# A chunked RWKV-7 recurrence: the triangular inverses and their products kept as 64x64 diagonal blocks, and grams of three slots

## The chip, the cores and the metric

The kernel runs on one core of one Trainium2 chip. The metric is the device time of one execution in microseconds (us), the median of several runs.

## What is computed

One layer of a hybrid streaming encoder for 1024 tokens of width 1024: input projection, a latent attention group, an RWKV-7 group, output projection, cross attention over 256 memory tokens, and a product-key expert stage. The change touches the RWKV-7 group alone. Of the reference, that is the scan below; each of its 8 heads has a state of 64x64 (the gates, decays and the group norm around it are left out here):

```python
def step(state, inp):
    r_t, w_t, k_t, v_t, kk_t, a_t = inp
    sa = jnp.einsum('bhvk,bhk->bhv', state, kk_t)
    state = (state * w_t[:, :, None, :]
             - sa[..., None] * (kk_t * a_t)[:, :, None, :]
             + v_t[..., None] * k_t[:, :, None, :])
    return state, jnp.einsum('bhvk,bhk->bhv', state, r_t)
```

## The kernel before

The program is a row of stages with a barrier of all engines between them, so the time of a stage is a part of the whole time. Inputs pass through input projection, the attention group, `rwkv_stage`, output projection, cross attention and the expert stage. Only `rwkv_stage` and its constant masks matter here.

`rwkv_stage` works on 8 tiles of 128 tokens. A tile holds two chunks of 64 tokens (CH) and 8 heads, as four pairs (PAIRS, index f) of an even and an odd head (index e). The scan over a chunk is turned into matrix products: for each head a lower triangular 64x64 matrix L has to be inverted, (I+L)^-1. The two chunks of a tile sit as the two diagonal blocks of a 128x128 matrix, whose other two blocks are zero, and all products are made on the 128x128 matrix.

A tile has two parts on each engine. `matrices` transposes four operands on TensorE (L980), then makes per head a "gram" of four 128x128 slots (L997, L999), which VectorE masks into `gm` (L1358) with `mask4`; its slot 2 keeps the pairs of neighbours alone, and from it the first step of the inverse is read (L1367). It makes the triangular matrix again, turned (L1006), which VectorE masks into `lb` (L1365) and into `yi` (L1374), then the bonus sum (L1013) and the products `ux` (L1018). ScalarE copies `ux` out (L1170).

`solve` doubles the inverted block size in five levels, l = 1 to 5. `xi` is the inverse (turned) and `yi` the same, unturned. Each level has three products per head: p = lb.xi (L1032), which ScalarE copies to `pe_s` (L1179); then z = yi.pe_s (L1048) and, but for the last level, its turned twin (L1051). VectorE copies from z the places of this level into `xi` (L1387, a copy under a mask) and from the twin into `yi` (L1389). The even heads (e = 0) and the odd heads (e = 1) go one behind the other: while ScalarE copies the even half, TensorE makes the odd one.

```python
for e in range(2):
    w.wait("p_taken", 2 * (l - 1) + e + 1)
    w.wait("inv_t", 2 * (l - 1) + e + 1)
    for f in range(PAIRS):
        last = nc.tensor.matmul(bank[2 + e][:, f, :], yi[e][:, f, :], pe_s[e][:, f, :], ...)
        if l < 5:
            last = nc.tensor.matmul(bank[4 + e][:, f, :], pe_s[e][:, f, :], yi[e][:, f, :], ...)
    inc(last, "z_mm")
```

After the levels, L1060 multiplies the inverse by the right sides, ScalarE copies the result to `nu` (L1189), L1068 to L1087 make what the states need, and L1094 and L1103 step the state through the two chunks. Every engine runs a program of its own, written out by hand, and waits on semaphores; `each_tile` loops over the tiles. The next tile's elementwise work (`prepare`, steps 0 to 6) is hung between the levels: TensorE makes step 1 (L952, L956) behind level 2 and step 3 (L963) in level 4, VectorE makes step 2 (L1301 to L1313) behind level 3 and step 4 (L1318 to L1331) behind level 5. GpSimd presets `yi` (L1263), makes the masks `level_t` when the stage begins (L1231 to L1243) and norms the tile before (L1217 to L1227).

All operands are float32. One matmul of the program shows as two LDWEIGHTS and two MATMUL records in the trace; "records" below are these. A form such as 64*128 128x128 names the rows and columns of the array that are in use, then partitions and columns of the moving operand.

## Time and profile before

| | us |
|---|---|
| median of 3 runs | 4144.01 |
| lowest and highest run | 4128.92, 4152.92 |
| the profiled execution's own time | 4149.77 |
| its span | 4148.2 |
| TensorE busy over the span | 3733.1 (90%) |
| VectorE, GpSimd, ScalarE busy | 2736.3, 1926.8, 1250.3 |

The trace gives the start and length of every instruction of one execution; a matmul's end is modelled, so lengths of matmuls overlap, and the distance between starts is what one costs. "Idle before" names what an engine waited for. PEclk is the granted clock of TensorE: 1.00 is the higher of its two levels (2.4 GHz) and 0.50 the lower (1.2 GHz).

### The profile page before, as it was taken

How to read it: one execution, taken by the hardware profiler on the slowest of the kernel's cores; microseconds unless marked ns; L12 is line 12 of the kernel's file. 1: busy time of each engine (PE TensorE's matmuls, PEld its weight loads, DVE VectorE, ACT ScalarE, POOL GpSimd, SP SyncE). 2: the span in 40 equal slices, each digit the busy share in tenths (PEclk: the TensorE clock that was granted, in tenths of full speed). 3: DMA queues.
4: the chain of work that ended last, by engine and by line, in shares of the span. 5: the costliest groups of instructions: out<-in, count | busy, mean ns of one | idle time of the engine just before them, and what ended most of it. 6: DMA issues, size and time to landing. Idle time of an engine off the chain costs nothing.

```text
span 4148.2 us, 54997 instructions
## 1 busy us (share of the span) xinstructions
PE 3733.1 (90%) x19168; PEld 3180.8 (77%) x19168; DVE 2736.3 (66%) x5219; ACT 1250.3 (30%) x1836; POOL 1926.8 (46%) x1352
## 2 busy tenths in 40 slices
PE   6958879999779789999999999999879988999998
PEld 5834468888667577889989999999657777778877
DVE  5453367777204437847778888878797655689986
ACT  2013234333102312133323333333233322433333
POOL 2004022222001001887878888888888888022220
PEclk9979889999899899999999999999989999999999
DMA  2229500000220023548878888888879888899995
GB/s 97 100 95 397 215 24 18 18 9 9 81 102 31 16 75 96 92 92 248 256 242 266 259 265 258 263 259 251 218 208 270 259 246 253 290 380 389 388 375 195
DMA packets 376334, 788.59 MB, mean 190 GB/s; under 512 B 137104, under 2 KB 245648, under 8 KB 342288
## 3 DMA queue, kind: packets, MB, share of 16 engines
q1 hardware_dynamic: 210320, 451.28, 31.9%
q0 software_dynamic: 165888, 336.01, 27.4%
q14 instruction: 93, 0.76, 0.1%
q8 instruction: 33, 0.54, 0.1%
HBM read 643.09 MB, written 144.05 MB: 190 GB/s over the span
## 4 chain that ended last, share of the span: by engine, by line
POOL 30%; PE 14%; issue 8%; DMA 4%; DVE 4%; ACT 1%; DVEq 1%; SPq 0%; POOLq 0%; ACTq 0%
POOL gates_d L2000 26%; PE peer_ps L2111 5%; PE peer_ps L2033 4%; PE peer_ps L2019 3%; DMA late_in<-gates_d 3%; POOL rows L1980 2%; POOL peer_rows L1980 2%; POOL late_rows L1980 1%; DVE late_rows L2389 1%; PE peer_ps L2057 1%; DVE peer_acc L2404 1%; DVEq L2403 1%; DMA rows<-in_expert_uv,peer_idx 1%; DMA peer_gat<-gates_d 1%; DMA peer_rows<-in_expert_uv,peer_idx 1%
## 5 line engine op out<-in xcount | busy, mean ns | idle before, releaser
L2000 POOL DMA_INDIRECT gates_d<-peer_gates,peer_idx x768 | 1343.9, 1750 | 325.8 <-issue 224.3
L2019 PE MATMUL peer_ps<-high,peer_uh 128*128 128x384 f32 x2048 | 532.5, 341 | 60.1 <-DVE peer_ul L2306 52.5
L2019 PE MATMUL peer_ps<-high,peer_ul 128*128 128x384 f32 x2048 | 527.3, 338 | 0.0
L2019 PE MATMUL peer_ps<-low,peer_uh 128*128 128x384 f32 x2048 | 527.2, 338 | 0.0
L2019 PEld LDWEIGHTS peer_ps<-high,peer_uh 128*128 128x128 f32 x2048 | 373.3, 191 | 73.5 <-issue 65.2
L2111 PE MATMUL peer_ps<-peer_vh,peer_ah 128*128 128x512 f32 x1026 | 331.4, 405 | 59.0 <-DVE peer_al L2423 58.4
L2019 PEld LDWEIGHTS peer_ps<-low,peer_uh 128*128 128x128 f32 x2048 | 376.5, 191 | 0.0
L2019 PEld LDWEIGHTS peer_ps<-high,peer_ul 128*128 128x128 f32 x2048 | 376.2, 191 | 0.0
L1980 POOL DMA_INDIRECT late_rows<-in_expert_uv,peer_idx x108 | 141.8, 1313 | 430.1 <-DVE peer_acc L2404 389.0
L2111 PE MATMUL peer_ps<-peer_vh,peer_al 128*128 128x512 f32 x1026 | 324.7, 398 | 0.0
L2111 PE MATMUL peer_ps<-peer_vl,peer_ah 128*128 128x512 f32 x1026 | 324.0, 398 | 0.0
L2157 ACT ACTIVATE peer_uh<-peer_raw 128x1024 fp32r<-128x1024 f32 x144 | 152.2, 1057 | 515.5 <-PE peer_ps L2019 436.1
L2111 PEld LDWEIGHTS peer_ps<-peer_vh,peer_ah 128*128 128x128 f32 x1026 | 194.4, 194 | 116.3 <-DVE peer_al L2423 75.5
L2111 PEld LDWEIGHTS peer_ps<-peer_vh,peer_al 128*128 128x128 f32 x1026 | 198.1, 193 | 43.7
L2111 PEld LDWEIGHTS peer_ps<-peer_vl,peer_ah 128*128 128x128 f32 x1026 | 197.6, 193 | 43.2
L2306 DVE TENSOR_TENSOR peer_ul<-peer_raw,peer_uh 128x1024 fp32r<-128x1024 f32 x144 | 177.2, 1230 | 78.6 <-ACT peer_uh L2157 62.8
L2111 PE MATMUL peer_ps<-peer_uh,peer_ah 128*128 128x512 f32 x510 | 165.1, 405 | 30.2 <-DVE peer_al L2423 29.7
L2196 ACT ACTIVATE peer_pre<-peer_pre 128x2 f32<-128x2 f32 x128 | 26.0, 203 | 516.3 <-DVE peer_pre L2389 512.8
L2389 DVE CUSTOM_DVE_ANT_0 late_rows<-late_rows,peer_xrow 128x1024 f32<-128x1024 f32 x108 | 128.3, 1219 | 60.3 <-DMA late_rows<-in_expert_uv,peer_idx 60.3
L2111 PE MATMUL peer_ps<-peer_uh,peer_al 128*128 128x512 f32 x510 | 163.0, 401 | 0.0
L2111 PE MATMUL peer_ps<-peer_ul,peer_ah 128*128 128x512 f32 x510 | 162.6, 400 | 0.0
L2404 DVE SCALAR_TENSOR_TENSOR peer_acc<-late_rows,peer_pre,peer_acc 128x1024 f32<-128x1024 f32 x108 | 138.8, 1285 | 9.5 <-issue 0.5
(442 smaller groups left out, 7609.6 us busy)
## 6 DMA issues: line engine op xcount, KB each, us to landing
late_in<-in_expert_uv SPq DMA_DIRECT2D x170, 512.0 KB
gates_d<-mla_zeros POOLq DMA_DIRECT2D x128, 512.0 KB
peer_raw<-in_expert_u SPq DMA_DIRECT2D x128, 512.0 KB
hidden_d<-peer_hid SPq DMA_DIRECT2D x128, 384.0 KB
peer_val<-in_expert_uv SPq DMA_DIRECT2D x86, 512.0 KB
late_in<-hidden_d SPq DMA_DIRECT2D x170, 192.0 KB
late_in<-gates_d SPq DMA_DIRECT2D x170, 192.0 KB
peer_act_in<-hidden_d SPq DMA_DIRECT2D x86, 192.0 KB
```

Source lines behind the costliest of these rows:

```text
L1980: pool.indirect_dma_start(buffer[:, :], None, expert_uv, bass.IndirectOffsetOnAxis(ap=idx[:, n, k:k + 1], axis=0)).then_inc(ready, 16)
L2000: pool.indirect_dma_start(gates_flat, bass.IndirectOffsetOnAxis(ap=idx[:, n, k:k + 1], axis=0), gates[:, n, k:k + 1], None, compute_op=ALU ...
L2019: last = nc.tensor.matmul(ps[i][:, a, 0:HD], w[:, cols], x[:, kc, a * HD:(a + 1) * HD], start=(kc == 0 and w is uh[i % 2] and x is high), ...
L2033: last = nc.tensor.matmul(ps[i][:, a, :], w[:, cols], x[:, kc, a * HALF:(a + 1) * HALF], start=(kc == 0 and w is uh[i] and x is high), sto ...
L2057: last = nc.tensor.matmul(ss[:, t, :], q[j % 2][:, t * P:(t + 1) * P], keys[:, j, :], start=True, stop=True)
L2111: last = nc.tensor.matmul(ps[n % 4][:, a, :], x[:, i * P:(i + 1) * P], w[:, a * HALF:(a + 1) * HALF], start=(first_block and x is ah[r] an ...
L2157: nc.scalar.activation(uh[b % 2][:, :], raw[b % 3][:, :], ACT.Copy).then_inc(u_high, 1)
L2196: nc.scalar.activation(pre[:, part], pre[:, part], ACT.Gelu).then_inc(gel_done, 1)
L2306: nc.vector.tensor_tensor(ul[b % 2][:, :], raw[b % 3][:, :], uh[b % 2][:, :].bitcast(F32), ALU.subtract).then_inc(u_low, 1)
L2389: nc.vector.tensor_tensor_reduce(out=buffer[:, 0:D], in0=buffer[:, 0:D], in1=xrow[row_place(p)[0]][:, :], scale=1.0, scalar=0.0, op0=ALU.m ...
L2403: dve.drain()
L2404: nc.vector.scalar_tensor_tensor(out=acc[tile][:, :], in0=rows(p)[0][:, D:2 * D], scalar=pre[:, p:p + 1], in1=acc[tile][:, :], op0=ALU.mul ...
```

## The change

`lb`, `xi`, `yi` and `pe_s` hold only the two diagonal blocks: 64 columns per head in place of 128, chunk 0 on partitions 0 to 63 and chunk 1 on 64 to 127. A product of a level is made as 16 matmuls of 64x64x64 in place of 8 of 128x128x128. A block of chunk c uses rows and columns 64c to 64c+63 of the array; `ROUNDS` puts a block of the even heads on one quarter beside a block of the odd heads on the quarter diagonal to it, each in a bank of its own. The even and the odd half are no longer staggered: one semaphore step per product. All `xi` copies of a level stand ahead of all `yi` copies. The gram has three slots (its second matmul has 128 columns in place of 256), and the first step of the inverse is read from a product of its own (`turned`). `level`, `lower` and `unit` are cut to blocks by GpSimd when the stage begins, and GpSimd presets `xi` too.

```diff
+        def in_bank(e, low=0):
+            return bank[e][:, low:low + 2, :].rearrange("p a (g c) -> p (a g) c", c=CH)
+        def chunk(c):
+            return slice(CH * c, CH * c + CH)
+        ROUNDS = (((0, 0), (1, 1)), ((0, 1), (1, 0)))
...
-                    inc(nc.tensor.matmul(bank[2 + h % 4][:, 2:4, :], bh[rows, f, :], ktrt[rows, f, :, :],
+                    inc(nc.tensor.matmul(bank[2 + h % 4][:, 2, :], bh[rows, f, :], ktrt[rows, f, 1, :],
...
                 for e in range(2):
-                    rows = slice(64 * e, 64 * e + 64)
                     w.wait("trans_taken", 3 + e)
+                pe.nop().then_inc(operands_seen, 1)
+                for turned in range(2):
                     for f in range(PAIRS):
-                        last = nc.tensor.matmul(bank[6 + e][:, f, :], ktrt[rows, f, 0, :], bh[rows, f, :],
-                                                start=True, stop=True)
+                        for c in range(2):
+                            for e in range(2):
+                                rows = slice(64 * e, 64 * e + 64)
+                                x, y = ktrt[rows, f, 0, chunk(c)], bh[rows, f, chunk(c)]
+                                last = nc.tensor.matmul(in_bank(6 + e, 2 * turned)[chunk(c), f, :], y if turned else x,
+                                                        x if turned else y, start=True, stop=True)
                     inc(last, "lb_mm")
...
+                def blocks(dst, x, y):
+                    pe.nop().then_inc(operands_seen, 1)
+                    for pair in ROUNDS:
+                        for f in range(PAIRS):
+                            for e, c in pair:
+                                rows = chunk(c)
+                                last = nc.tensor.matmul(in_bank(dst + e)[rows, f, :], x[e][rows, f, :], y[e][rows, f, :],
+                                                        start=True, stop=True)
+                    return last
...
-                    for e in range(2):
-                        w.wait("p_taken", 2 * (l - 1) + e + 1)
-                        w.wait("inv_t", 2 * (l - 1) + e + 1)
-                        for f in range(PAIRS):
-                            last = nc.tensor.matmul(bank[2 + e][:, f, :], yi[e][:, f, :], pe_s[e][:, f, :],
-                                                    start=True, stop=True)
-                            if l < 5:
-                                last = nc.tensor.matmul(bank[4 + e][:, f, :], pe_s[e][:, f, :], yi[e][:, f, :],
-                                                        start=True, stop=True)
-                        inc(last, "z_mm")
+                    w.wait("p_taken", 2 * l)
+                    w.wait("inv_t", 2 * l)
+                    inc(blocks(2, yi, pe_s), "z_mm")
+                    if l < 5:
+                        inc(blocks(4, pe_s, yi), "z_mm")
...
-                    for f in range(PAIRS):
-                        last = nc.tensor.matmul(bank[e][:, f, :], xi[e][:, f, :], rhsU[:, 2 * f + e, :],
-                                                start=True, stop=True)
-                    inc(last, "u_mm")
+                    for f in range(PAIRS):
+                        for e, c in pair:
+                            rows = chunk(c)
+                            last = nc.tensor.matmul(bank[e][rows, f, :], xi[e][rows, f, :], rhsU[rows, 2 * f + e, :],
+                                                    start=True, stop=True)
+                inc(last, "u_mm")
...
-                        inc(nc.scalar.activation(flat(pe_s[e]), flat(bank[e]), ACT.Copy), "p_taken")
+                        inc(nc.scalar.activation(pe_s[e][:, :, :], in_bank(e), ACT.Copy), "p_taken")
...
-                gv = gm[:, :, :, :].rearrange("p (f e) w c -> p f e w c", e=2)
+                w.wait("lb_mm", 2)
                 for e in range(2):
-                    w.wait("lb_mm", e + 1)
-                    inc(nc.vector.tensor_tensor(lb[e][:, :, :], bank[6 + e][:, :, :], over_heads(consts["lower"][:, :]),
-                                                ALU.mult), "lb")
-                    inc(nc.vector.tensor_tensor(xi[e][:, :, :], gv[:, :, e, 2, :], over_heads(consts["ident"][:, :]),
-                                                ALU.add), "inv")
+                    inc(nc.vector.tensor_tensor(lb[e][:, :, :], in_bank(6 + e), over_blocks(lower[:, :]), ALU.mult), "lb")
+                w.wait("preset", 4)
+                dve.nop().then_inc(blocks_seen, 1)
+                for e in range(2):
+                    inc(nc.vector.copy_predicated(xi[e][:, :, :], where(level_t, 0), in_bank(6 + e, 2)), "inv")
...
+                    for n, (dst, masks, src, done) in enumerate(((xi, level_t, 2, "inv"), (yi, level, 4, "inv_t"))):
+                        if l == 5 and n:
+                            continue
+                        w.wait("z_mm", 2 * l - 1 + n)
+                        dve.nop().then_inc(blocks_seen, 1)
+                        for e in range(2):
+                            inc(nc.vector.copy_predicated(dst[e][:, :, :], where(masks, l), in_bank(src + e)), done)
```

How the instructions stand. First TensorE in level 4 of the loop over tiles: p, then step 3 of the next tile, then the start of z and its twin. Before (a row without "x" is one matmul of the program):

```order
L1032 MATMUL rwkv_bank<-rwkv_xi,rwkv_lb 128x128 [waits rwkv_inv]
L1032 MATMUL rwkv_bank<-rwkv_xi,rwkv_lb 128x128 x3
L902 REGISTER_ALU
L1032 MATMUL rwkv_bank<-rwkv_xi,rwkv_lb 128x128 [waits rwkv_inv]
L1032 MATMUL rwkv_bank<-rwkv_xi,rwkv_lb 128x128 x3
L902 REGISTER_ALU
L963 MATMUL rwkv_bank<-rwkv_sqk,headones 128x512 [waits pin_rstd_ready,pin_scaled_ready]
L902 REGISTER_ALU
L1048 MATMUL rwkv_bank<-rwkv_pe_s,rwkv_yi 128x128 [waits rwkv_inv_t,rwkv_p_taken]
L1051 MATMUL rwkv_bank<-rwkv_yi,rwkv_pe_s 128x128
```

The same place in the changed kernel, to the end of the twin:

```order
L1046 MATMUL rwkv_bank<-rwkv_xi,rwkv_lb 64x64 [waits rwkv_inv]
L1046 MATMUL rwkv_bank<-rwkv_xi,rwkv_lb 64x64 x15
L912 REGISTER_ALU
L973 MATMUL rwkv_bank<-rwkv_sqk,headones 128x512 [waits pin_rstd_ready,pin_scaled_ready]
L912 REGISTER_ALU
L1046 MATMUL rwkv_bank<-rwkv_pe_s,rwkv_yi 64x64 [waits rwkv_p_taken,rwkv_inv_t]
L1046 MATMUL rwkv_bank<-rwkv_pe_s,rwkv_yi 64x64 x15
L1046 MATMUL rwkv_bank<-rwkv_yi,rwkv_pe_s 64x64 x16
```

Each product is now 16 small matmuls behind one wait; z stands whole ahead of its twin.

Second, VectorE behind level 3, with step 2 of the next tile and the copies of level 4. Before:

```order
L1387 COPY_PREDICATED rwkv_xi<-rwkv_level_t,rwkv_bank 128x512 [waits rwkv_z_mm]
L1389 COPY_PREDICATED rwkv_yi<-level,rwkv_bank 128x512
L1301 SCALAR_TENSOR_TENSOR rwkv_cum<-scanmask,rwkv_sgw 128x512 [waits pin_sq_summed]
L1303 TENSOR_TENSOR rwkv_prev<-rwkv_cum,rwkv_sgw 128x512
L1305 TENSOR_TENSOR rwkv_rem<-rwkv_cum 128x512
L1310 SCALAR_TENSOR_TENSOR rwkv_ta<-rwkv_al,cols 128x512 [waits pin_sq_summed]
L1313 SCALAR_TENSOR_TENSOR rwkv_k<-rwkv_ta,rwkv_rkv 128x512
L902 REGISTER_ALU
L1387 COPY_PREDICATED rwkv_xi<-rwkv_level_t,rwkv_bank 128x512 [waits rwkv_z_mm]
```

And in the changed kernel:

```order
L1415 COPY_PREDICATED rwkv_xi<-rwkv_level_t,rwkv_bank 128x256 [waits rwkv_z_mm]
L1415 COPY_PREDICATED rwkv_xi<-rwkv_level_t,rwkv_bank 128x256
L912 REGISTER_ALU
L1415 COPY_PREDICATED rwkv_yi<-rwkv_level,rwkv_bank 128x256 [waits rwkv_z_mm]
L1415 COPY_PREDICATED rwkv_yi<-rwkv_level,rwkv_bank 128x256
L1329 SCALAR_TENSOR_TENSOR rwkv_cum<-scanmask,rwkv_sgw 128x512 [waits pin_sq_summed]
L1331 TENSOR_TENSOR rwkv_prev<-rwkv_cum,rwkv_sgw 128x512
L1333 TENSOR_TENSOR rwkv_rem<-rwkv_cum 128x512
L1338 SCALAR_TENSOR_TENSOR rwkv_ta<-rwkv_al,cols 128x512 [waits pin_sq_summed]
L1341 SCALAR_TENSOR_TENSOR rwkv_k<-rwkv_ta,rwkv_rkv 128x512
L912 REGISTER_ALU
L1415 COPY_PREDICATED rwkv_xi<-rwkv_level_t,rwkv_bank 128x256 [waits rwkv_z_mm]
```

The copies have half the columns, and step 2 still stands whole between the copies of level 3 and those of level 4.

## Rows read from the trace of the kernel before

**Rows 1.** Busy time by stretch (stretch, length, PE, PEld, DVE, ACT, POOL)
```profile
570.00:1040.00 470.00, 443.41 (x3720) 404.81 (x3718) 339.47 (x464) 175.55 (x273) 115.83 (x100) 0.99 0.05 14
682.20:743.20 61.00, 57.09 (x482) 51.79 (x480) 45.77 (x62) 23.94 (x38) 16.25 (x14) 1.00 0.06 15
```
**Rows 2.** Timeline of TensorE, one tile (start, length, line, form, records)
```profile
664.04 1.16 PE L1068 MATMUL rwkv_bank<-rwkv_br_t,rwkv_nu 64*128 64x128 f32 x8 [0.69 <-ACT rwkv_nu L1189]
...
673.46 1.10 PE L1094 MATMUL rwkv_bank<-rwkv_q,rwkv_state 128*128 128x64 f32 x8 [1.31 <-DVE rwkv_q L1406]
...
682.72 0.71 PE L997 MATMUL rwkv_bank<-rwkv_ktrt,rwkv_kh 64*128 64x256 f32 x4
...
691.07 2.16 PE L1032 MATMUL rwkv_bank<-rwkv_xi,rwkv_lb 128*128 128x128 f32 x16
...
698.01 2.38 PE L1032 MATMUL rwkv_bank<-rwkv_xi,rwkv_lb 128*128 128x128 f32 x16 [0.32 <-DVE rwkv_xi L1387]
...
705.88 2.05 PE L1032 MATMUL rwkv_bank<-rwkv_xi,rwkv_lb 128*128 128x128 f32 x16
...
711.40 2.26 PE L1032 MATMUL rwkv_bank<-rwkv_xi,rwkv_lb 128*128 128x128 f32 x16
...
717.99 2.39 PE L1032 MATMUL rwkv_bank<-rwkv_xi,rwkv_lb 128*128 128x128 f32 x16
722.21 2.11 PE L1060 MATMUL rwkv_bank<-rwkv_rhsU,rwkv_xi 128*128 128x128 f32 x16
725.01 1.16 PE L1068 MATMUL rwkv_bank<-rwkv_br_t,rwkv_nu 64*128 64x128 f32 x8 [0.69 <-ACT rwkv_nu L1189]
```
**Rows 3.** Timeline of TensorE: narrow matmuls, and matmuls on parts of the array
```profile
666.38 0.27 PE L1073 MATMUL rwkv_bank<-rwkv_v_t,rwkv_kr_t 64*128 64x128 f32 x1
666.38 0.37 PE L1068 MATMUL rwkv_bank<-rwkv_br_t,rwkv_nu 64*128 64x128 f32 x1
...
669.26 1.09 PE L1081 MATMUL rwkv_bank<-rwkv_gm,rwkv_nu 128*64 128x128 f32 x16
...
689.34 1.89 PE L1018 MATMUL rwkv_bank<-rwkv_v_t,rwkv_gm 128*128 128x64 f32 x16
```
**Rows 4.** Weight loads by line and form (busy, mean ns of one)
```profile
L1060 PEld LDWEIGHTS rwkv_bank<-rwkv_rhsU,rwkv_xi 128*128 128x128 f32 x128 | 15.4, 191 | 1.4 <-DVE rwkv_xi L1387 1.4
...
L1085 PEld LDWEIGHTS rwkv_bank<-rwkv_gm,rwkv_v_t 128*64 128x64 f32 x128 | 10.5, 146 | 0.0
```
**Rows 5.** Timeline of ScalarE, the same tile
```profile
691.27 0.60 ACT L1170 ACTIVATE rwkv_rhsU<-rwkv_bank 128x512 f32<-128x512 f32 x1 [6.17 <-PE rwkv_bank L1018]
691.88 1.28 ACT L1179 ACT_TABLE_LOAD   x1
693.17 1.08 ACT L1179 ACTIVATE rwkv_pe_s<-rwkv_bank 128x512 f32<-128x512 f32 x2
```
**Rows 6.** Timeline of VectorE, the same tile
```profile
683.88 4.87 DVE L1358 TENSOR_TENSOR rwkv_gm<-rwkv_bank,mask 128x512 f32<-128x512 f32 x8 [3.13 <-PE rwkv_bank L999]
...
712.34 0.73 DVE L1389 COPY_PREDICATED rwkv_yi<-level,rwkv_bank 128x512 f32<-128x512 uint32 x1
...
717.17 0.76 DVE L1387 COPY_PREDICATED rwkv_xi<-rwkv_level_t,rwkv_bank 128x512 f32<-128x512 uint32 x1 [0.28 <-issue]
```
**Rows 7.** TensorE and its granted clock (next to last but two) where it fell
```profile
907.20:910.60 3.40, 2.71 (x26) 2.62 (x27) 3.30 (x2) 1.63 (x3) 2.04 (x2) 0.99 0.00 0
910.60:920.90 10.30, 10.30 (x76) 9.79 (x74) 8.61 (x12) 0.00 (x0) 2.05 (x2) 0.51 0.00 0
```
**Rows 8.** Timeline of TensorE in that tile
```profile
907.98 1.16 PE L1068 MATMUL rwkv_bank<-rwkv_br_t,rwkv_nu 64*128 64x128 f32 x8 [0.69 <-ACT rwkv_nu L1189]
...
920.89 1.10 PE L1094 MATMUL rwkv_bank<-rwkv_q,rwkv_state 128*128 128x64 f32 x8
```
**Rows 9.** Timeline of GpSimd as the stage begins
```profile
533.53 0.24 POOL L1243 TENSOR_SCALAR_AFFINE_SELECT rwkv_level_t<-rwkv_level_t 128x64 f32<-128x64 f32 x1
537.02 1.04 POOL L1205 TENSOR_TENSOR rwkv_kkr<-rwkv_rkv,cols 128x512 f32<-128x512 f32 x1 [3.25 <-DMA rwkv_gd<-feats_d]
```

More of the change, by code:

```diff
@@ L138, in _ @@
             nc.gpsimd.memset(low[:, :], 1.0).then_inc(made, 1)
-            nc.gpsimd.memset(m4[:, 2, :], 0.0).then_inc(made, 1)
-            n = 12
-            for i in (0, 1, 3):
+            n = 11
+            for i in range(3):
                 pool.wait_ge(made, n)
                 nc.gpsimd.affine_select(out=m4[:, i, :], in_=m4[:, i, :], compare_op=ALU.is_ge, fill=0.0,
-                                        base=-1 if i % 2 == 0 else 0, pattern=[[1, P]],
+                                        base=0 if i else -1, pattern=[[1, P]],
                                         channel_multiplier=-1).then_inc(made, 1)
@@ L848, in rwkv_stage, with blocks4 @@
         kr_t, br_t, v_t = (tile4(x) for x in ("kr_t", "br_t", "v_t"))
-        gm = st.sb("gm", [P, 2 * PAIRS, 4, P])
-        lb = [tile4(f"lb{e}") for e in range(2)]
-        xi = [tile4(f"xi{e}") for e in range(2)]
-        yi = [tile4(f"yi{e}") for e in range(2)]
-        level_t = st.sb("level_t", [P, 6, P])
+        gm = st.sb("gm", [P, 2 * PAIRS, 3, P])
+        def blocks4(name):
+            return st.sb(name, [P, PAIRS, CH])
+        lb, xi, yi, pe_s = ([blocks4(f"{x}{e}") for e in range(2)] for x in ("lb", "xi", "yi", "pe_s"))
+        level, level_t = st.sb("level", [P, 6, CH]), st.sb("level_t", [P, 6, CH])
+        unit, lower = st.sb("unit", [P, CH]), st.sb("lower", [P, CH])
         bonus_kept, gate_kept = tile4("bonus_kept"), tile4("gate_kept")
-        pe_s = [tile4(f"pe_s{e}") for e in range(2)]
         nu = st.sb("nu", [P, 2, 2 * PAIRS, 64])
@@ L1080, in solve @@
                     f, rows = h // 2, slice(64 * (h % 2), 64 * (h % 2) + 64)
-                    last = nc.tensor.matmul(bank[4][rows, f, :], nu[:, 0, h, :], gm[:, h, 3, :], start=True, stop=True)
+                    last = nc.tensor.matmul(bank[4][rows, f, :], nu[:, 0, h, :], gm[:, h, 2, :], start=True, stop=True)
                 inc(last, "q_mm")
@@ L1086, in solve @@
                                      start=(h < 2), stop=False, skip_group_check=True)
-                    nc.tensor.matmul(bank[5][rows, f, :], nu[:, 1, h, :], gm[:, h, 3, :],
+                    nc.tensor.matmul(bank[5][rows, f, :], nu[:, 1, h, :], gm[:, h, 2, :],
                                      start=False, stop=False, skip_group_check=True)
@@ new lines, in made @@
+                def made(ins):
+                    nonlocal n
+                    n += 1
+                    ins.then_inc(masks_made, 1)
+                    pool.wait_ge(masks_made, n)
+                for c in range(2):
+                    rows = chunk(c)
+                    made(nc.gpsimd.tensor_tensor(level[rows, :, :], consts["level"][rows, :, rows],
+                                                 ones[rows, 0:CH].unsqueeze(1).broadcast_to([CH, 6, CH]), ALU.mult))
+                    for dst, src in ((lower, consts["lower"]), (unit, consts["ident"])):
+                        made(nc.gpsimd.tensor_tensor(dst[rows, :], src[rows, rows], ones[rows, 0:CH], ALU.mult))
@@ new lines, in make_masks @@
+                made(nc.gpsimd.memset(level_t[:, :, :], 1.0))
+                for l in range(6):
+                    b = 1 << l
+                    for c in range(2):
+                        v = level_t[chunk(c), l, :].rearrange("p (j y) -> p j y", y=2 * b)
+                        made(nc.gpsimd.memset(v[:, :, 0:b], 0.0))
+                        for base, step in ((0, -1), (b - 1, 1)):
+                            made(nc.gpsimd.affine_select(out=v[:, :, b:2 * b], in_=v[:, :, b:2 * b], fill=0.0,
+                                                         compare_op=ALU.is_ge, base=base,
+                                                         pattern=[[2 * step * b, CH // (2 * b)], [0, b]],
+                                                         channel_multiplier=-step))
@@ L1260, in matrices @@
                 if before:
-                    before.wait("u_mm", 2)
-                for e in range(2):
-                    inc(nc.gpsimd.tensor_tensor(yi[e][:, :, :], over_heads(consts["ident"][:, :]),
-                                                over_heads(consts["ident"][:, :]), ALU.mult), "preset")
+                    before.wait("u_mm", 1)
+                for x in xi + yi:
+                    inc(nc.gpsimd.tensor_tensor(x[:, :, :], over_blocks(unit[:, :]), over_blocks(unit[:, :]), ALU.mult),
+                        "preset")
                 if before:
@@ L2522, in build @@
         front = ctx.enter_context(ExitStack())
[L2523 removed]
+        for name, shape in (("headones", [P, P]), ("rot", [ROPE, P]), ("gram_masks", [P, 3, P]), ("level", [P, 6, P]),
                             ("lower", [P, P]), ("scanmask", [P, 4 * P])):
```

86 lines of the change are left out of this document (29 added, 57 removed).

## The prediction

> **What bounds the kernel now.** I read busy time by stretch first. Over the RWKV loop TensorE is busy 443 of 470 us, and in one tile 57.1 of 61.0; VectorE is busy 45.8 and ScalarE 23.9 [rows 1]. So TensorE carries the loop, and what it waits for is small. The timeline of TensorE gives the tile its stretches [rows 2]: first gram to p of level 1, 8.35 us (682.72 to 691.07); then 6.94 to level 2, 7.87 to level 3, 5.52 to level 4, 6.59 to level 5, 4.22 to the product with the right sides (u, L1060) and 2.80 to L1068. A tile takes 60.97 (664.04 to 725.01), so from L1068 to the next first gram 18.7 remain. In the levels TensorE stands in one of two states: it streams, 2.1 to 2.4 us for 16 records of p, or it waits briefly for a copy (0.32 before p of level 2).
>
> **The price of one small record.** Everything hangs on r, the distance between starts of two records in a stream of 64x64x64 blocks that alternate between two diagonal quarters. No row shows such a block. The rows around it [rows 2, 3, 4]:
> - A full 128x128 record with 128 columns: (2.11 - 0.27) / 16 = 115 ns, u. With 64 moving columns (L1018) (1.89 - 0.27) / 15 = 108. So halving the moving columns brings next to nothing; the weight load sets the distance.
> - A load of 64 columns takes 146 ns in place of 191, 45 less. A block on its own quarter would take 108 - 45 = 63.
> - Work on two halves of the array runs side by side: L1068 and L1073 on the two row halves start both at 666.38, and L1081 on the two column halves starts a record each (1.09 - 0.27) / 15 = 54.5 ns, half of 108. The shortest steady distance anywhere in the trace is that 54.5.
>
> So r is 63 / 2 = 31 if both effects join, 54.5 if the halves' pace is a limit of issue, and 27 if the load shrinks in proportion (54.5 / 2). I take 31: the two effects are shown apart, and nothing in the rows says that they exclude each other.
>
> The Trainium skill ("TensorE: Matmul & The Clock Gate", LDWEIGHTS) has a load take its columns divided by 1.2 in ns, so 53 for 64 columns and, by two, 27 per record; with it the sum would be 1.6 us per tile lower, an estimate. The 191 and 146 of the rows do not fall in that proportion.
>
> **The change part by part**, per tile.
>
> A block product is 32 records: 31 x 0.031 + 0.27 = 1.23 us. The copies have 256 columns in place of 512: VectorE's 0.73 to 0.76 [rows 6] lies between 0.37 and 0.76 afterwards, I take 0.47, and 0.36 between starts; ScalarE's two copies of 1.08 together [rows 5] become 0.67. Hand-overs I put at 0.05 to ScalarE and 0.05 back, 0.15 to VectorE and 0.06 back, an estimate from starts and ends that stand next to each other in the same timelines. Then:
> - p to z: 1.23 + 0.05 + 0.67 + 0.05 = 2.00. z to the next p: 1.23 + 0.15 + 0.83 + 0.06 = 2.27. A level is 4.27. The twin (0.99) runs beside the xi copies, and the level could end no sooner than 2.00 + 1.98 by TensorE.
> - First gram to p of level 1. VectorE's eight masks pace the grams, 4.87 / 8 = 0.61 each [rows 6], and with 384 columns 0.46 to 0.47: 1.15 saved. The second product of each gram has half the columns. Against it, the turned product makes 64 records where L1006 had 16, and p waits for all of `lb` and `xi`, which wait for all 64. 8.75 for 8.35: **+0.4**.
> - Level 1: p, then ScalarE copies ux (0.60), loads its table (1.28) and only then copies p [rows 5], so z starts 2.7 after p; 1.0 for z, 1.04 for copies, and a drain of 0.1: 4.9 for 6.94, **-2.05**.
> - Level 2: 4.27, and TensorE's step 1 of the next tile behind it (0.3) and the wait for the twin, 6.26 for 7.87: **-1.6**.
> - Levels 3 and 4: VectorE's step 2 is unchanged, 713.07 to 717.17, 4.10 [rows 6], and still stands between the copies of level 3 and the `xi` copies of level 4. With yi done 5.1 after p of level 3, step 2 4.1 and xi 0.95, p of level 5 comes 10.15 after p of level 3, for 12.11: **-1.96**. Here TensorE idles for VectorE, about 1.5 us that it did not idle before.
> - Level 5 to u: 4.27 for 4.22, **+0.05**. With TensorE short, ScalarE and VectorE no longer hide behind the other half. The stagger was worth what the small blocks give.
> - u keeps 128 moving columns: 32 records on two quarters, 2.0 for 2.1, but one semaphore for both halves, so both copies to `nu` stand behind it: 3.15 for 2.80, **+0.35**.
> - L1068 onward nothing is changed but its start. The wait of 1.31 before L1094 is for VectorE [rows 2], which has been relieved by more than TensorE: **-1.3**.
>
> Sum: 0.4 - 2.05 - 1.6 - 1.96 + 0.05 + 0.35 - 1.3 = **-6.1 per tile**. Seven tiles and a last one worth 5.5 give -48.
>
> GpSimd makes 43 mask operations where it made 16, up to 533.77. The last took 0.24 [rows 9]; at 0.3 each with a wait behind every one, 27 more are some 8 us, of which 3.25 is already a wait for a DMA. `kkr` comes some 5 us later. Its result goes to steps that start behind others; 0, at most +3 once. The two further presets (256 columns for 512) keep GpSimd's time per tile, 16.3 of 61 [rows 1]: 0.
>
> The clock. Once in the loop it fell [rows 7]: behind the stretch at 907.2, in which TensorE was busy 2.71 of 3.40 with L1068 on 64 rows, it stood at 0.51 for 10.3 us. From L1068 to L1094 that tile took 12.91 [rows 8] where another takes 9.42 [rows 2], so a fall costs 3.5. Afterwards a longer wait stands before L1068, and u before it uses half the rows at a time. I estimate three more falls: **+10.5**.
>
> Sum 4149.8 - 48 + 10.5 = 4112 for an execution like the profiled one, which lies 5.8 above the median; so **4107** for the median, 0.9% below 4144.01. What a measurement can tell from no change is about 0.5%, 20.7 us: faster is below 4123, slower above 4165.
>
> **The price of a miss in r.** p, z and part of the twin stand on the path, about 410 records of the 512 small ones per tile, so 0.41 us per tile for each ns. With r = 27 and no further falls: -7.7 per tile, 4082. The gain reaches 0.5% for r below 36, the sign turns, falls included, at 43, and the loss reaches 0.5% at 49.
>
> **The rivals.**
> 1. *The middle*: r between 37 and 49, since pairs start side by side only in part (each matmul is two records on the same quarter, one behind the other), or a drain at each change from quarters to the whole array. For it: r has to undercut the shortest distance of the trace by 15 to 30% only. At r = 43 the tile gains 6.1 - 4.9 = 1.2, the falls take that, and it ends at 4144.
> 2. *Issue-bound*, slower: records stay 54.5 apart, as in the column halves. A product then takes 32 x 0.0545 = 1.96, about what it took before, while the stagger is gone and copies lie bare on the path: -6.1 + 23.5 x 0.41 = +3.5 per tile, +28, with the falls +38.5: 4183. For it: nothing in the trace is closer than 54.5. Against it: two rows start at the same 666.38.
> 3. *The clock*: a stream on two of four quarters, with waits of 0.8 to 1 us twice per level, lets it fall in the levels too. Small records at 0.5 cost at least what rival 2 has (+3.5), and L1068 to L1094 3.5 more, so +7 per tile: 4200. It decides from the first tile whose levels run at 0.5. For it: the fall followed half-row work beside 0.69 of idle [rows 7, 8]. Against it: in the loop half-row work stands in every tile, and the clock fell in one.
> 4. *Quarters do not run together at all* (weights of one quarter wait for the other): r = 63, +7 per tile, with the falls 4210.
>
> The Trainium skill ("TensorE: Matmul & The Clock Gate", back-to-back issue gap) has a case in which each MATMUL costs 62 ns of sequencer whatever its size; that would be rival 2 at its hardest, or rival 4 in effect. The trace's 54.5 speaks against it. Its page "TensorEngine Tiling (Array Packing)", Instruction Overhead, also warns that a matmul of 1 moving column lasts as long as one of 60; no row here goes below 64.
>
> **How the numbers follow.** Forecast (r up to 36, few falls) 0.48; the middle 0.24; issue-bound 0.16; clock 0.09; no overlap 0.03. Of the middle, 0.02 still ends faster by over 0.5%: faster 0.50, same 0.22, slower 0.28. The range takes r = 27 at one end and the issue-bound case at the other, 4085 to 4185; outside are the clock and no-overlap cases and a few better ones. The forecast's own range is 4085 to 4123.
>
> **What would show it.** In the changed trace: a p of 32 records with starts over 1.0 us (right), 1.7 (rival 2), 2.0 (rival 4); p of level 4 to p of level 5 longer than that of level 3 to 4, with TensorE idle for VectorE's step 2; p of level 1 to p of level 2 near 4.9; the tile at 55; a granted clock of 0.5 behind L1068 in three or four tiles of eight. The prediction is wrong if r is above 36, if the clock falls within the levels, or if VectorE's copies of 256 columns cost as much as those of 512.

## The result, and the profile of the changed kernel

The changed kernel took 4172.34 us in the median of 18 runs, the one before 4148.44 in as many; the ratio is 1.006 with a 95% interval of 1.0044 to 1.0076. It is slower by 0.6%. Forecast was 0.9% faster. All traces below are of one execution each; those of the two kernels took 4149.77 and 4172.61 us.

The same stretch of the RWKV loop as in [rows 1], of the changed kernel (stretch, length, busy time of PE, PEld, DVE, ACT and POOL, granted clock, DMA share, GB/s):

```profile
570.00:1040.00 470.00, 381.59 (x5799) 340.44 (x5799) 278.98 (x452) 151.51 (x270) 123.98 (x113) 0.86 0.06 15
```

TensorE, which was busy 443 of 470 us, is busy 382, and its clock has gone from 0.99 to 0.86. So the work shrank, as it should, and something else fills the time: waits, and work at the lower clock. The view of waits names the waits. TensorE in the whole stage (engine, tile and line that waited, what it waited for, total us, times, longest):

```profile
PE rwkv_bank L1046 <- issue: 26.6, 11, 3.9
PE rwkv_bank L1046 <- ACT rwkv_pe_s L1198: 23.1, 25, 0.9
PE rwkv_bank L1046 <- DVE rwkv_xi L1415: 13.8, 21, 1.6
...
PE rwkv_bank L1087 <- ACT rwkv_nu L1208: 9.5, 8, 1.2
```

The first row does not exist in the kernel before: 26.6 us, 25.0 of them in eight waits of 2.5 to 3.9 us, in which TensorE waited for nothing that a semaphore or a transfer of data explains. The timeline of TensorE shows where, at the first product of level 1 of a tile, and there in pairs:

```profile
685.06 1.89 PE L1033 MATMUL rwkv_bank<-rwkv_v_t,rwkv_gm 128*128 128x64 f32 x16
689.65 0.24 PE L1046 MATMUL rwkv_bank<-rwkv_xi,rwkv_lb 64*64 64x64 f32 x1 [2.70 <-issue]
693.54 1.97 PE L1046 MATMUL rwkv_bank<-rwkv_xi,rwkv_lb 64*64 64x64 f32 x31 [3.65 <-issue]
695.44 2.04 PE L1059 MATMUL rwkv_bank<-rwkv_gd,rwkv_g_up 128*128 128x128 f32 x8
```

Its inputs were there (VectorE ended the last `xi` copy at 685.7 and the bonus product at 686.3). TensorE waits 2.70 us, makes one record, waits 3.65 more, and then runs at half the clock: 1.97 for 31 records (granted 0.50 from 693.5 to 695.5). This is the first matmul of the loop's body, to which TensorE jumps back. Of the six jumps back, four have it; I call it a stop below. The part of the page on DMA queues has the other half of the evidence: q8, a queue of kind "instruction", moved this in the whole program of before (transfers, MB, share of 16 engines):

```profile
q8 instruction: 33, 0.54, 0.1%
```

and this in the changed one:

```profile
q8 instruction: 74, 1.21, 0.1%
```

Asked for the stretch from 640 to 1000 us, the middle of the loop, the queue shows 35 transfers after the change,

```profile
q8 instruction: 35, 0.57, 0.7%
```

and before the change it has no row there at all, so I read that TensorE's body stayed on the chip from pass to pass. The same view, asked pass by pass, ties the stops to the transfers: 8 or 9 transfers in each pass that begins with a stop (8 from 684 to 740), and 1 in each of the two that do not (1 from 740 to 805).

One tile that the code did not disturb, on TensorE, is what the prediction's stretches can be held against:

```profile
747.66 0.71 PE L1007 MATMUL rwkv_bank<-rwkv_ktrt,rwkv_kh 64*128 64x256 f32 x4
...
755.34 1.15 PE L1046 MATMUL rwkv_bank<-rwkv_xi,rwkv_lb 64*64 64x64 f32 x32
...
760.36 1.15 PE L1046 MATMUL rwkv_bank<-rwkv_xi,rwkv_lb 64*64 64x64 f32 x32 [0.16 <-DVE rwkv_xi L1415]
...
766.43 1.15 PE L1046 MATMUL rwkv_bank<-rwkv_xi,rwkv_lb 64*64 64x64 f32 x32
...
772.88 1.15 PE L1046 MATMUL rwkv_bank<-rwkv_pe_s,rwkv_yi 64*64 64x64 f32 x32
773.87 1.10 PE L1046 MATMUL rwkv_bank<-rwkv_yi,rwkv_pe_s 64*64 64x64 f32 x32
776.59 1.15 PE L1046 MATMUL rwkv_bank<-rwkv_xi,rwkv_lb 64*64 64x64 f32 x32 [1.62 <-DVE rwkv_xi L1415]
...
780.90 1.96 PE L1079 MATMUL rwkv_bank<-rwkv_rhsU,rwkv_xi 64*64 64x128 f32 x32 [1.08 <-DVE rwkv_xi L1415]
784.06 1.16 PE L1087 MATMUL rwkv_bank<-rwkv_br_t,rwkv_nu 64*128 64x128 f32 x8 [1.19 <-ACT rwkv_nu L1208]
```

z begins at 772.88 and its twin at 773.87, so 32 small records take 0.99 us, 31 ns each: r came out at the value taken. A tile with a stop takes 68.2 to 68.5 us from L1087 to L1087, an undisturbed one 58.2. Even the shorter is 3.3 above the forecast's 54.9, and that is the clock. By stretch (columns as above), the 10 us up to an L1087, the 13.6 behind it, and the 13.6 behind the next L1087:

```profile
647.80:658.00 10.20, 5.36 (x119) 4.79 (x116) 6.82 (x11) 4.96 (x10) 3.98 (x5) 1.00 0.00 0
658.00:671.60 13.60, 13.60 (x105) 13.20 (x104) 9.50 (x13) 0.41 (x1) 3.16 (x4) 0.62 0.00 0
...
726.00:739.60 13.60, 13.60 (x103) 13.21 (x104) 9.26 (x12) 0.88 (x2) 4.97 (x5) 0.62 0.00 0
```

TensorE is busy 5.36 of the 10.2 us up to L1087, and then the clock is 0.62 over 13.6 us. It is so behind all eight L1087, where before it fell in one tile [rows 7]. The clock also falls within level 5 of each tile that had a stop. z of level 5 and u in one of them,

```profile
717.97 1.97 PE L1046 MATMUL rwkv_bank<-rwkv_pe_s,rwkv_yi 64*64 64x64 f32 x32 [0.94 <-ACT rwkv_pe_s L1198]
721.03 3.68 PE L1079 MATMUL rwkv_bank<-rwkv_rhsU,rwkv_xi 64*64 64x128 f32 x32 [1.08 <-DVE rwkv_xi L1415]
```

take 1.97 and 3.68 where the undisturbed tile has 1.15 and 1.96. So a tile with a stop can hold three falls: at the stop, in level 5, and behind L1087.

### The profile page after: what moved, and what is told of

Same layout as the page of the kernel before. It is cut to its first block, busy times and chain, and to the rows that moved or that the text cites. A ratio compares the mean times of both kernels' runs of the same rounds, so it can differ in the third digit from the quotient of the medians.

```text
span 4170.7 us, 59519 instructions
## 1 busy us (share of the span) xinstructions
PE 3690.5 (88%) x21472; PEld 3128.5 (75%) x21472; DVE 2681.5 (64%) x5219; ACT 1229.0 (29%) x1836; POOL 1945.5 (47%) x1392
## 4 chain that ended last, share of the span: by engine, by line
POOL 29%; PE 11%; issue 8%; DMA 6%; DVE 5%; ACT 2%; DVEq 1%; SPq 0%; POOLq 0%; ACTq 0%
POOL gates_d L2025 25%; DMA late_in<-gates_d 4%; PE peer_ps L2058 4%; PE peer_ps L2044 3%; PE peer_ps L2136 3%; POOL rows L2005 2%; POOL peer_rows L2005 2%; POOL late_rows L2005 1%; DVE peer_acc L2429 1%; DMA peer_rows<-in_expert_uv,peer_idx 1%; DVE late_rows L2414 1%; DMA rows<-in_expert_uv,peer_idx 1%; DVEq L2428 1%; PE peer_ps L2082 1%; DVE peer_al L2448 1%
```

## The experiments

Two theories were on the table, for two different losses. F: TensorE's longer body no longer stays on the chip, and its code is fetched behind the jump back. C: the clock falls behind L1087 because TensorE idles at four places ahead of it (before and behind p of level 5, before and behind u). The rival to F was that the idle belongs to the load of the next tile's inputs, which runs at the same moment (768 KB, issued at 686.56), or to the small blocks themselves. All kernels but e2 and e3 start from the changed one. Ratios are against the kernel before, on the same chip.

**e1: TensorE's loop written out.**

```diff
-            with eng.Fori(0, NT - 1) as t:
-                this, following = Tile(eng, t), Tile(eng, t, 1)
-                ...
+            for t in range(NT - 1):
+                this, following = Tile(eng, t), Tile(eng, t, 1)
+                ...
```

> The changed kernel, with TensorE's loop over tiles written out (7 tiles of code in place of one and a jump back); nothing else differs. Theory F (code): the changed kernel's idle of 2.70 + 3.65 us at the first product of level 1, in four of seven passes of the loop, is TensorE waiting for its own code after the jump back, since the body with 768 records per tile no longer stays on the chip (74 transfers of code in queue q8 where before has 33). Without a jump the idle goes: every tile takes about 58.2 us, the four long ones lose 10 us each, 4172 - 41 = about 4131; the clock still falls behind the product with the right sides. Rival R (data): the idle comes from the load of the next tile's inputs, 768 KB, that runs at the same moment, or from a wait that the trace does not name; then tiles of 68.2 us stay and the time is 4172.

Measured: 4126.07, ratio 0.9954 (0.9931 to 0.9978). (The other engines keep their loop.) The stops at the first product are gone from the timeline, and q8 moves 74 transfers as before: as much code as in the changed kernel, fetched ahead of need in place of behind a jump. The load of the inputs is still there, issued at 687.80 in the pass where p of level 1 starts without a wait at 688.13, so the rival of the load falls; and the small blocks are still there, so that one falls too. In the trace, from the first L1087 to the last (L1101 here), 596.55 to 1009.97 = 413.4 us for the changed kernel's 599.20 to 1042.96 = 443.8. So the code cost 30.3 us in these two executions. That is a net figure: the four tiles with a stop were 10.0 to 10.3 longer each, 40.5 together, and e1 has three tiles of 60.4 to 62.2 among its 58.2, in which the clock fell in level 5 as well. The medians lie 46.3 apart.

**e2: the loop written out in the kernel before.** Same edit.

> The kernel before, with TensorE's loop over tiles written out. Control for e1: before shows no idle at a jump back, so theory F expects no gain, 4148 plus or minus 8 and tiles of 61.0 us. Rival R expects the same. If it gains as much as e1, writing the loop out brings something else than what is claimed for it.

Measured: 4154.28, ratio 1.0012 (0.9995 to 1.003), tiles of 60.9 to 61.0, and a last one with a fall of the clock. Writing out is worth nothing where the body was resident.

**e3: the kernel before with a loop body of two tiles.**

```diff
-            with eng.Fori(0, NT - 1) as t:
-                tile(t)
+            with eng.Fori(0, (NT - 1) // 2) as half:
+                tile(2 * half)
+                tile(2 * half + 1)
+            tile(NT - 2)
```

> The kernel before, with TensorE's loop made over two tiles at a time (three passes, and the seventh tile behind them), so the body of the loop is twice as long while every matmul is that of before. Theory F: with some 2,000 instructions the body does not stay on the chip, so idle of several us that no other engine ends appears at the jump back, in two or three places, and queue q8 shows over 50 transfers; 15 to 30 us slower than before. Rival R (the idle belongs to the small blocks or to the data): no such idle, same time as before.

Measured: 4154.84, ratio 1.0017 (0.9999 to 1.0035). By time this is a miss: 15 to 30 us were expected, 4.9 came by the medians (0 to 15 by the interval). By mechanism it is a hit. TensorE alone has the new loop, and its timeline has, at the first of the two jumps back,

```profile
693.27 2.05 PE L1046 MATMUL rwkv_bank<-rwkv_xi,rwkv_lb 128*128 128x128 f32 x16 [1.83 <-issue]
```

and at the second

```profile
816.12 2.05 PE L1046 MATMUL rwkv_bank<-rwkv_xi,rwkv_lb 128*128 128x128 f32 x16 [1.52 <-issue]
```

and q8 has 61 transfers. No block of 64 is in this kernel, and its data transfers are those of before; the load of the next inputs is issued at 692.46, when the first of these waits has lasted 1.0 us. So a long body alone brings the idle. The tiles around the jumps take 62.2 and 61.9 for 61.0, no more, and the clock stays at 1.00. So the length of the body decides whether there is a stop, and something else how long it is; in the changed kernel there are two waits in a row, here one. Why was not settled. One rival stands: in the changed kernel the load is issued at 686.56, ahead of the wait, and its 768 KB move while the code is fetched; no run separates the two.

**e4: e1, and TensorE's waits filled.** Matmuls of two constants into a bank that is free there (for which step 3 of the next tile also waits for `biased` 2 in place of 1, here and in every kernel with a filling):

```diff
+                def fill(n):
+                    for _ in range(n):
+                        nc.tensor.matmul(bank[7][:, 0, :], consts["ident"][:, :], consts["ident"][:, :],
+                                         start=True, stop=True)
...
+                    if l == 5:
+                        fill(6)
                     w.wait("inv", 2 * l)
                     inc(blocks(0, lb, xi), "p_mm")
+                    if l == 5:
+                        fill(4)
...
+                fill(4)
                 w.wait("inv", 12)
...
                 inc(last, "u_mm")
+                fill(4)
```

> e1, and matmuls of two constants into a bank that nobody reads then, where TensorE waits before the end of the levels: 6 (12 records of 128x128) ahead of p of level 5, 4 behind it, 4 ahead of u and 4 behind u. Theory C (clock): the fall to 0.5 at each L1087 comes from TensorE's idle of 0.9 to 1.6 us at four places within the 10 us before; filled, the clock stays at 1.00 and a tile takes 58.2 - 3.5 = 54.7 us, which is 28 us below e1. Rival: the clock falls nevertheless, since small records count little; then e4 is as e1, or up to 5 us slower by what the filling delays.

Measured: 4089.26, ratio 0.9858 (0.9808 to 0.9909). Every tile but the last takes 54.0 us, and the last, which prepares none, 51.5. By stretch, the loop, then the time around u, and behind L1087 (L1112 here, at 700.79):

```profile
570.00:1000.00 430.00, 377.67 (x6152) 333.80 (x6148) 283.68 (x460) 153.18 (x272) 124.71 (x117) 0.99 0.06 17
...
694.00:702.00 8.00, 7.90 (x111) 7.12 (x108) 5.13 (x5) 2.78 (x6) 2.81 (x5) 1.00 0.01 2
702.00:713.00 11.00, 9.68 (x111) 9.12 (x109) 10.46 (x15) 0.00 (x0) 2.97 (x3) 1.00 0.00 0
```

L1112 runs from 592.74 to 968.34, 375.6 us, 37.8 less than in e1. C holds: useless work, put into the waits, buys 38 us. Some 28 of them are the falls behind u (six tiles of 54.0 for 58.2, the last 51.5 for 54.3) and some 10 the three falls in level 5.

**e10, e11: which waits.** The filling of e4 only at u (`fill(4)` ahead and behind), or only around p of level 5.

> e4 with the filling ahead of u and behind u alone (4 and 4 matmuls), none around p of level 5. If the clock falls for the two waits around u, it stays at 1.00 and e10 is as e4 (4089). If the emptier stretch around p of level 5 counts as well, some tiles fall and e10 lies near 4105.

Measured: 4092.68, ratio 0.9872 (0.9835 to 0.9909). Four tiles take 53.3 to 53.9, two, with a fall in level 5, 56.6 to 56.7, the last 50.1. None has a fall behind u.

> e4 with the filling around p of level 5 alone (6 ahead, 4 behind), none around u. If the waits around u are what lets the clock fall, e11 is as e1 (4126). If any stretch filled is enough, it is as e4 (4089).

Measured: 4112.30, ratio 0.9928 (0.9906 to 0.995). Two tiles take 54.0 and four 58.26 (the last 51.5), nothing between: a fall behind u costs 4.2 us. So each group of waits alone can bring falls, and those around u weigh more: by time e10 can't be told from e4. Neither expectation for e11 was right, the truth lies between them.

**e6: e4, with the same blocks but without neighbours on different quarters.**

```diff
-        ROUNDS = (((0, 0), (1, 1)), ((0, 1), (1, 0)))
+        ROUNDS = (((0, 0), (1, 0)), ((0, 1), (1, 1)))
```

> e4 with the order of blocks changed alone: the even and the odd head's block of the same chunk follow each other on the same quarter, so no two neighbours can run side by side. If the side-by-side work on two quarters is what makes a record cost 29 to 31 ns, p now lasts 32 x 0.062 = 2.0 us in place of 1.0, and a tile is 8 to 12 us longer than e4's 54.0 (4150 to 4180 in all). If small records are cheap for their size alone, nothing changes.

Measured, in one run: 4308.4, where 4150 to 4180 was expected. TensorE makes the same p once at the full clock and, a level on, at the half clock:

```profile
723.32 1.90 PE L1065 MATMUL rwkv_bank<-rwkv_xi,rwkv_lb 64*64 64x64 f32 x32
...
741.16 3.30 PE L1065 MATMUL rwkv_bank<-rwkv_xi,rwkv_lb 64*64 64x64 f32 x32
```

At the full clock it is 1.90 where pairs on two quarters take 1.15, so the starts are (1.90 - 0.22) / 31 = 54 ns apart and not 30: side by side work is what makes the small record cheap. The 0.75 us come 14 times per tile, an estimate of 10.5 us, within what was expected; but the first five tiles take 82.3 to 85.2 for 54.0. Much of the rest is the clock, which the expectation left out, by stretch:

```profile
729.00:760.00 31.00, 29.16 (x299) 26.93 (x298) 9.60 (x20) 9.62 (x17) 9.44 (x9) 0.56 0.00 1
```

TensorE counts as busy 29.16 of 31 us and is granted 0.56. The lower clock makes work longer, so that share says little by itself; but from 700 to 729, at 1.00, it was busy 27.56 of 29, and the fall came at 732.5. The prediction's rival of a clock that falls within the levels is there with this order of blocks, from level 2 on in the tile shown; in the changed kernel the clock falls in level 5, and in level 1 behind a stop.

**e7: e4 with four slots again.** The gram's second matmul back to 256 columns, masks over 512.

```diff
-                    inc(nc.tensor.matmul(bank[2 + h % 4][:, 2, :], bh[rows, f, :], ktrt[rows, f, 1, :],
+                    inc(nc.tensor.matmul(bank[2 + h % 4][:, 2:4, :], bh[rows, f, :], ktrt[rows, f, :, :],
...
-                    inc(nc.vector.tensor_tensor(gm[:, h, :, :], bank[2 + h % 4][:, 0:3, :], consts["gram_masks"][:, :, :],
+                    inc(nc.vector.tensor_tensor(gm[:, h, :, :], bank[2 + h % 4][:, :, :], consts["gram_masks"][:, :, :],
```

> e4 with one part undone: the gram has four slots again (second matmul of 256 columns, masks over 512 columns), slot 2 unused. By the prediction the three slots save VectorE 8 x 0.145 = 1.15 us per tile ahead of p of level 1. So e7 is 8 to 9 us slower than e4, 55.1 us per tile. If the grams are hidden, it is as e4.

Measured: 4095.07, ratio 0.987 (0.9849 to 0.989), 5.8 above e4, whose interval it overlaps; the trace is sharper. Tiles of 55.1 for 54.0, and on VectorE in e7

```profile
671.04 4.87 DVE L1411 TENSOR_TENSOR rwkv_gm<-rwkv_bank,gram_masks 128x512 f32<-128x512 f32 x8 [3.13 <-PE rwkv_bank L1023]
```

where e4 has

```profile
665.26 3.81 DVE L1411 TENSOR_TENSOR rwkv_gm<-rwkv_bank,gram_masks 128x384 f32<-128x384 f32 x8 [2.92 <-PE rwkv_bank L1023]
```

1.06 us for eight masks, and all of it reaches the tile's period (1.09).

**e8: e4's filling in the changed kernel's loop.**

> The changed kernel, loop and all, with e4's filling. The clock and the code come apart: if both losses add, the stalls at the jump back stay (about 6 us each, in four or more passes) and the falls behind u go, so the time lies between e4 and the changed kernel, 4172 - 28 = about 4144. The filling makes the body 36 instructions longer, which may bring a stall in every pass: then up to 4165. If the clock falls behind a stall as well, 10 us per stalled tile remain.

Measured: 4144.33, ratio 0.9991 (0.9972 to 1.0011). Tiles of 61.4 to 62.1, so 7.4 to 8.1 above e4's, and all six jumps back now stop. The 4144 that was expected is met in part by luck: it stood for four stops. The two stops of one of them:

```profile
681.10 0.24 PE L1051 MATMUL rwkv_bank<-rwkv_xi,rwkv_lb 64*64 64x64 f32 x1 [1.77 <-issue]
685.50 1.97 PE L1051 MATMUL rwkv_bank<-rwkv_xi,rwkv_lb 64*64 64x64 f32 x31 [4.16 <-issue]
```

The two losses come apart: the filling takes away the falls in level 5 and behind u, and the stops remain, each with a fall of the clock at it. The body is longer by 36 records and their loads, and the stop comes every time.

**e9 and e5: the stagger put back.** The two chunks of one head stand side by side, and the even heads run ahead of the odd ones again:

```diff
-                def blocks(dst, x, y):
+                def blocks(dst, x, y, e):
                     pe.nop().then_inc(operands_seen, 1)
-                    for pair in ROUNDS:
-                        for f in range(PAIRS):
-                            for e, c in pair:
+                    for f in range(PAIRS):
+                        for c in range(2):
...
-                    inc(blocks(2, yi, pe_s), "z_mm")
-                    if l < 5:
-                        inc(blocks(4, pe_s, yi), "z_mm")
+                    for e in range(2):
+                        w.wait("p_taken", 2 * (l - 1) + e + 1)
+                        w.wait("inv_t", 2 * (l - 1) + e + 1)
+                        inc(blocks(2, yi, pe_s, e), "z_mm")
+                    if l < 5:
+                        for e in range(2):
+                            inc(blocks(4, pe_s, yi, e), "z_mm")
```

(p, u and the engines that wait for them in the same way; the loop written out as in e1. e5 has a smaller filling besides.)

> e4 with the stagger of before put back: the blocks of the even heads, then those of the odd heads, each half with its own semaphore step in p, z, the twin and u; the two chunks of one head stand side by side on the diagonal quarters, in one bank. ScalarE copies the even half while TensorE makes the odd one. Filling: 6 ahead of p of level 5, 1 behind it, 3 ahead of u, 3 behind it. If ScalarE's bare wait (0.94 us per level in the changed kernel) is what the single semaphore step costs, levels 1, 2 and 5 gain near 1 us each, levels 3 and 4 together near 1, and u 0.5: 54.0 - 4 = about 50 us per tile, 30 us below e4, 4060. If two quarters into one bank do not run side by side, a block record costs 62 ns in place of 29 and e5 is slower than e4.

Measured: 4062.04, ratio 0.9797 (0.9777 to 0.9816), tiles of 50.9.

> e5 without any filling. If the stagger alone takes enough of TensorE's idle away, the clock stays at 1.00 and e9 is as e5, 4062, or a little below, since nothing is multiplied in vain. If it does not, a fall of 3 to 4 us comes in some or all tiles, and e9 lies between e5 and e5 + 30, near 4085.

Measured: 4058.19, ratio 0.9796 (0.976 to 0.9832), five tiles of 50.3 to 50.6, one of 54.3 and the last of 45.9. TensorE's timeline in e9:

```profile
718.41 1.15 PE L1059 MATMUL rwkv_bank<-rwkv_xi,rwkv_lb 64*64 64x64 f32 x32
719.75 1.15 PE L1059 MATMUL rwkv_bank<-rwkv_pe_s,rwkv_yi 64*64 64x64 f32 x32 [0.19 <-ACT rwkv_pe_s L1214]
720.70 1.13 PE L1059 MATMUL rwkv_bank<-rwkv_yi,rwkv_pe_s 64*64 64x64 f32 x32
...
729.88 1.96 PE L1095 MATMUL rwkv_bank<-rwkv_rhsU,rwkv_xi 64*64 64x128 f32 x32 [0.27 <-DVE rwkv_xi L1431]
732.53 1.16 PE L1103 MATMUL rwkv_bank<-rwkv_br_t,rwkv_nu 64*128 64x128 f32 x8 [0.69 <-ACT rwkv_nu L1224]
```

Two quarters that write into one bank run side by side as well (z to its twin 0.95 us). The wait for `pe_s` is 0.19 for 0.94, that before u 0.27 for 1.08, that before L1103 0.69 for 1.19. No filling is needed: the stagger by itself gives the clock back in all but the tile of 54.3 (0.54 from 837 to 847). This also answers a rival to C, that the filling helped by its kind of work, on the whole array, and not by ending the idle: e9 adds no work. e5 and e9 can't be told apart by time; they are the fastest kernels of the study, 2.0% under the one before.

**e12: e9 with the loop kept.**

> The changed kernel with the stagger of e9 and its loop as it stands, not written out. Theory F: the body is as long as in the changed kernel, so the idle at the jump back returns in four to seven passes, 6 us of idle each and 10 if the clock falls behind it: 4058 + 25 to 60, so 4083 to 4120. Rival: with the staggered order the fetch is hidden and it is as e9.

Measured: 4115.63, ratio 0.994 (0.9919 to 0.9961), tiles of 57.9 to 58.7. The view of waits of its stage begins

```profile
PE rwkv_bank L1045 <- issue: 38.0, 13, 4.2
```

F again: the same order of work, 57 us slower for its jump back. Here all six jumps stop without any filling. The body has some 15 instructions more than the changed kernel's, so little decides between four stops and six, or it is not the length alone.

## Why the prediction was wrong

Two steps of the prediction failed: the body's code, which no term of its sum stood for, and the clock, of whose falls it expected three more. Over the seven intervals from L1068 (L1087) of the first tile to that of the last, before takes 1029.68 - 603.08 = 426.6 and the changed kernel 443.8. The runs split the 17.2 between:

| | us | from |
|---|---|---|
| blocks, gram, order of the halves, no fall of the clock (the filling's own time included) | -51.0 | e4 375.6 for 426.6 |
| falls of the clock behind u and in level 5 | +37.8 | e1 413.4 for e4 375.6 |
| TensorE waiting for its code | +30.3 | changed 443.8 for e1 413.4 |

The two executions differ by 22.8 in all. The other 5.6 is made of 3.9 less ahead of the first L1087 and 9.5 more behind the last. What stands there is the end of the last tile and the stages that no kernel changes, and it takes 3115 to 3131 us in the traces of this study, whatever the kernel; so I put nothing of the 9.5 down to the change.

*Right: the price of a record.* 31 ns was taken, 30 to 31 measured, and e6 shows that it rests on the two quarters. The exact hit has luck in it: 31 was half of 63 for one quarter, and one quarter alone measures 54, of which two quarters save less than half. Rivals 1, 2 and 4 are out. Rival 3, the clock, came true in part, in level 5 and behind the stops.

*Right: the sum of the stretches*, in the undisturbed tile: first gram to p 7.68 (8.75 forecast, 8.35 before); level 1 5.02 (4.9); level 2 6.07 (6.26); levels 3 and 4 10.16 (10.15, with TensorE idle 1.62 for VectorE's step 2, as said); level 5 4.31 (4.27); u 3.16 (3.15). (The working of level 2 names 4.27, 0.3 and a wait; its 6.26 holds only with the 1.98 us of TensorE's step 1, L952 at 703.90 to p at 705.88 before, in it.) The one term with the wrong sign was the first: +0.4 was forecast for the matrices and -0.67 came. The masks saved 1.06 of the 1.15 forecast (e7), so what is left comes mostly from the turned product: the 64 records of L1021 take 1.1 us, where 64 at 31 ns would be 2.0. (They stand on quarters of all four kinds, each starting beside its neighbour: 32 in 0.52, 16 ns each, half of what a level's record costs.) From there to the next gram, unburdened in e4, is 17.5 for 18.7, where 1.3 was taken off. The tile without falls is 54.0, its filling included, against the 54.9 forecast. One slip changed nothing: rival 2's product is written as 32 x 0.0545 = 1.96, and that is 1.74; 1.96 is 31 x 0.0545 + 0.27.

*Wrong by size: the clock.* "I estimate three more falls: +10.5." Its mechanism was named (a longer wait ahead of L1068, half-array work), its cost per fall too (3.5; e11 shows 4.2), but not its number: with the one of before it stood for four, and there were eight behind L1087, five in level 5 and four at the stops. What the step overlooked is that the waits of the levels and those around u belong together. The prediction had itself worked out that ScalarE's and VectorE's copies would lie bare, some 0.9 to 1.6 us at a time, and priced them as time alone. e10 and e11 show that both groups count. With +38 in place of +10.5 the forecast would have been 4134, no longer clearly faster and not slower. What exactly has to come together before a fall is not shown.

*Wrong by omission: the code.* No term of the sum stood for it. "Each product is now 16 small matmuls" was read as a price per record and never as 288 more records, and as many weight loads, in the body of a loop. The sign of the result hangs on this step: e1 differs from the changed kernel in it alone, and is on the other side of the kernel before. The Trainium skill ("Runtime: NRT & Kernel Launch", Instruction fetch mechanics) has the mechanism: code comes in blocks of 16 KiB, and a taken branch to what is not held makes the engine wait for a transfer. The q8 rows agree (0.54 MB in 33 transfers is 16 KB each). It also gives TensorE's memory 2,048 instructions; by that rule the changed body, some 1,536 matmul records and loads with a few dozen others, should have stayed, and here it did not at four jumps of six. (The same section speaks of a window of two blocks, by which neither body would stay; the one of before, some 960, stayed, with no transfer from 640 to 1000.) Before the change the trace held what could have been read as a warning: q8 was quiet there, so the length of 960 was known to be safe and any greater length was not.

*Luck: the range.* 4172 lies inside the stated 4085 to 4185, but its upper end was the issue-bound case, records 54.5 apart, and that did not come. The code and the falls beyond the fourth brought the time there, and the range had neither.

*Rightly put at nothing:* GpSimd's masks. It ends them at 541.9 in place of 533.8 and starts `kkr` 5.0 us later, at 542.01, as forecast; the first gram comes at 559.98 for 560.47 before, so the delay reached nothing.

## What to carry to other kernels

A change that splits one instruction into several changes the length of the code as well as the work: where an engine runs a loop, compare its body to what stayed resident before (no transfers of kind "instruction" in the loop), and write the loop out, or keep the body short, before judging the change. A faster engine with the same partners idles more, and on TensorE idle can be paid twice, once as time and once as clock; so a speed-up and a coarser hand-over should not be put in together. Here, from e1's 58.2 us per tile, filling the waits brought 54.0 and halves that overlap brought 50.3.

## What the runs showed of the hardware

- Records of 64x64x64 blocks on two diagonal quarters start 30 to 31 ns apart, on one quarter 54 ns (e6); into one bank or two makes no difference (0.95 us from z to its twin in e9, 0.95 to 0.99 in the changed kernel). Where all four quarters take part and two neighbours never share rows (L1021), 32 records take 0.52 us.
- The clock does not follow the busy share of the records alone: e6, in its one run, has TensorE busy 27.56 of the 29 us up to 729 and 29.16 of the 31 behind it, with levels on one quarter at a time, and falls to 0.50 at 732.5. A tile of e9, with pairs on two quarters and a smaller busy share, keeps 1.00:

```profile
712.00:762.00 50.00, 44.26 (x765) 38.98 (x762) 38.62 (x62) 21.87 (x37) 16.23 (x17) 1.00 0.07 19
```

- A single wait for code is 1.5 to 4.4 us, and one stop has one (e3) or two in a row (5.7 to 6.4 us together in the other loops). It comes at a jump back and not in straight code, even with 76 transfers in the program (e4), so fetching ahead kept up with a stream of 31 ns records there.
- Open: why two passes of the changed loop kept their code (1 transfer each) and the others fetched 8 or 9, and why a body of two tiles of before waits only 1.5 to 1.8 us per jump.
